# Second unit's gate remainder on GpSimd, first down weights one place sooner, first code products of the extra units behind a gate/up product

## Chip, cores and metric

The kernel runs on 1 core of one Trainium2 chip. The metric is the device time in microseconds of one execution; for a kernel it is the median of its runs.

## What is computed

One layer of a hybrid encoder on x (1, 512, 1024) in float32: RMSNorm, one input projection, a chunked gated delta rule and a sliding-window attention beside each other, a gated merge with output projection and residual, then a mixture of experts. The change lies in the mixture:

```python
grp_prob = jax.nn.softmax(t @ w_rg + b_rg); grp_p, grp_idx = lax.top_k(grp_prob, 1)
top_logits, top_local = lax.top_k(in_group, TOP_K_IN_GROUP)        # 4 groups of 4 experts, 2 experts a token
weights = grp_p * jax.nn.softmax(top_logits, axis=-1)
for gi in range(N_EXPERT_GROUPS):
    act = jax.nn.silu(t @ w_gate[e]) * (t @ w_up[e])                # D_FF_EXPERT = 256
    out = out + (act * combine[:, e, None]) @ w_down[e]
```

followed by the residual and a last RMSNorm.

## The kernel before

Every float32 product is made of three products of rounded parts: a high part (fp32r, copied by ScalarE) and a remainder (raw less high, by VectorE). `three` (lines 1713 to 1716) issues hi·hi, lo·hi and hi·lo, so a weight tile is of use to TensorE (PE) only when ScalarE has made its high part and VectorE (DVE) its remainder.

**Units.** The experts' work is cut into UNITS = 23 units of up to 128 tokens: the 16 experts' first tokens, and 7 extra units for experts with more than 128. `SEQ` gives their order; the first four are experts 0 to 3. For a unit u the kernel gathers its tokens (`fetch`, line 722, GpSimd's queue, an indirect DMA of 128 rows), turns them (`unit_in`, line 2130, PE), splits them (`split_in_hi` on ScalarE, `split_in_lo` on DVE, line 1582), multiplies by gate and up (`gate_up`, 24 products of 128x512), applies SiLU (ScalarE) and the product with up (DVE, line 1634), turns the hidden values (`hidden_f`), splits them (lines 1085 and 1645), and multiplies by down (`down`, 12 products). The loop is a pipeline written out by hand: PE's place u holds unit_in(u+1), the first half of gate_up(u), hidden_f(u-1), the second half of gate_up(u), down(u-1).

**Weights.** Each of a unit's three matrices comes in two loads of 512 KB into a ring of eight raw slots (`ew_raw`). `place` gives a matrix its place c in the order of loads (gate 0, up 0, gate 1, up 1, gate 2, down 0, up 2, gate 3, down 1, ...) and from it the slot and a running count. A load into a slot waits until the remainder of what lay there is made: `elo_done` counts the remainders in the order of the places. SyncE (SP) issues the loads of the 16 experts in program order; GpSimd gathers those of the extra units by row numbers that the routing yields.

**Routing.** Between the residual and the first unit stands the routing, on DVE in small steps chained by a semaphore each. For batches of experts it builds one-hot rows (`one_hots`, line 1550), PE multiplies them with token codes (`row_codes`, line 2110), and DVE turns the result into row numbers (`row_ids`, lines 1557 and 1558). Batches 0 to 4 are the experts (`EARLY` = 5), batches 5 to 8 the extra units, which are made inside the unit loop: `extra_units` in DVE's place 0, `row_codes(5)` to `row_codes(8)` in PE's places 1 to 4 ahead of gate_up(u).

Behind `row_ids(3)` DVE forms the tokens' weights in five small instructions (lines 1572 to 1578), then `row_ids(4)`, then:

```python
1580            split_expert_lo(KIND_G, 1)
...
1626            split_in_lo(0)
1627            split_expert_lo(KIND_U, 1)
```

and in the loop, at place u: the product with up of unit u-1, the remainder of gate u+1, split_in_lo(u+1), (place 0: extra_units), the remainder of down u-1, hidden_lo, the remainder of up u+1, and at places 1 to 4 `row_ids` and `one_hots` of the extra batches.

Of the kernel before, what the change touches and what calls it, by code (L numbers as in the profile page):

```python
# [14 lines left out]
F32 = mybir.dt.float32  # L15
# [67 lines left out]
def build(nc, a, out):  # L83
# [14 lines left out]
    with ctx:  # L98
# [267 lines left out]
        pool_set = sem("gpsimd_set")  # L366
        IDENT_SET, CONSTS, DIST_SET, ROUTE_CONSTS, ZERO_SET, SUB_DONE = range(1, 7)
        choice_step = sem("choice_step")
# [110 lines left out]
        for c in range(3 * UNITS):  # L479
            if c < 4:  # L480
                owner = c // 2
            elif c >= 3 * UNITS - 2:
                owner = c - 2 * UNITS
            else:
                owner = ((c + 2) // 3, (c - 5) // 3, c // 3)[(c + 2) % 3]
            for half in range(2):
                n = 2 * c + half
                LOADS.append((owner, n % EXPERT_RING))
# [19 lines left out]
        def place(kind, u, half=1):  # L508

            if kind == KIND_G:  # L510
                c = 3 * u - 2 if u > 1 else 2 * u
            elif kind == KIND_U:
                c = 3 * u if u > 1 else 2 * u + 1
            else:
                c = 3 * u + 5 if u < UNITS - 2 else 3 * UNITS - (UNITS - u)
            n = 2 * c + half
            return n % EXPERT_RING, (16 if SEQ[u] < NE else 32) * LOADS[n], n + 1

        def halves(gu, kind):
# [37 lines left out]
        def _(sp):  # L557
# [58 lines left out]
            def load(kind, u):  # L616
                if SEQ[u] >= NE:
                    return
                for half in range(2):
                    slot, _, count = place(kind, u, half)  # L620
                    if count > EXPERT_RING:

                        sp.wait_ge(elo_done, count - EXPERT_RING)
                    src = (w_gate_v, w_up_v, w_down_v)[kind][SEQ[u]]
                    src = src[:, half, :] if kind == KIND_D else src[:, UH * half:UH * (half + 1)]
                    sp.dma_start(eraw[slot][:, :], src).then_inc(eraw_in[slot], 16)
# [4 lines left out]
            for t in range(TT):  # L631
                if t < TT - 1:
                    sp.wait_ge(t_scaled, t + 1)
                else:
                    sp.wait_ge(choice_exp, ROW_SCALED)
                sp.dma_start(h_rows[t * P:(t + 1) * P, :], tx[t][:, :]).then_inc(rows_out, 16)
            for u in range(1, UNITS - 1):
                load(KIND_G, u + 1)
                load(KIND_D, u - 1)
                load(KIND_U, u + 1)  # L640
# [16 lines left out]
        def _(pool):  # L657
# [75 lines left out]
            def load_extra(kind, u):  # L733
# [5 lines left out]
                for half in range(2):  # L739
                    slot, _, count = place(kind, u, half)  # L740
                    pool.wait_ge(elo_done, count - EXPERT_RING)
                    c = 2 * (kind == KIND_D) + half
                    nc.gpsimd.indirect_dma_start(
                        out=eraw[slot][:, :], out_offset=None, in_=weight_rows[kind],
                        in_offset=bass.IndirectOffsetOnAxis(ap=wix[:, x_, c:c + 1], axis=0),
                        bounds_check=2 * P * NE - 1, oob_is_err=False).then_inc(extra_in[slot // 2], 16)
# [9 lines left out]
            pool.wait_ge(rows_out, 16 * TT)  # L756
            for u in range(4):
                fetch(u)
            for u in range(UNITS):
# [18 lines left out]
        def _(act):  # L778
# [285 lines left out]
            for u in range(UNITS + 1):  # L1064
# [11 lines left out]
                if u == 0:  # L1076
                    act.wait_ge(tt_ps, WEIGHTS_TURNED)
                    act.activation(w12_f[:, :], ps[1][0:2 * TT, 0:P], ACT.Copy).then_inc(choice_exp, 1)
                    act.wait_ge(choice_exp, WEIGHTS_COPIED)
                    act.dma_start(wt_rows[:, :].rearrange("(r p) o -> r (p o)", p=P), w12_f[:, :]).then_inc(slots_out, 16)  # L1080
                if u:
                    if u < UNITS:
                        split_expert(KIND_D, u - 1)
# [20 lines left out]
        def _(dve):  # L1104
# [474 lines left out]
            row_ids(4)  # L1579
            split_expert_lo(KIND_G, 1)  # L1580

# [47 lines left out]
            for u in range(UNITS + 1):  # L1629
                if u:  # L1630
                    dve.wait_ge(gsilu, u)
                    if u >= 3:
                        dve.wait_ge(hidt_ps, u - 2)
                    dve.tensor_tensor(ea[(u - 1) % 2][:, :], eg[:, :], ps[(u - 1) % 2][:, FF:], ALU.mult).then_inc(hid_done, 1)
                if 0 < u < UNITS - 1:
                    split_expert_lo(KIND_G, u + 1)
# [4 lines left out]
                if u:  # L1641
                    if u < UNITS:
                        split_expert_lo(KIND_D, u - 1)
# [68 lines left out]
        def _(pe):  # L1712
# [444 lines left out]
            def down(u):  # L2157
                pe.wait_ge(elo_done, place(KIND_D, u)[2])
                pe.wait_ge(hid_lo, u + 1)
# [13 lines left out]
            for u in range(UNITS):  # L2173
# [5 lines left out]
                if u == 1:  # L2179
                    pe.wait_ge(choice_exp, WEIGHTS_COPIED)  # L2180
                if 1 <= u <= 4:
                    row_codes(EARLY + u - 1)
                pe.wait_ge(elo_done, place(KIND_U, u)[2])
                pe.wait_ge(xs_lo_done, u + 1)
# [3 lines left out]
                if u:  # L2188
                    hidden_f(u - 1)
                gate_up(u, range(KT // 2, KT))  # L2190
                if u:
                    down(u - 1)
# [46 lines left out]
```

## Time and profile before

| | us |
|---|---|
| median of 3 runs (681.89 to 683.1) | 682.11 |
| the profiled execution's own time | 682.08 |
| its span, from the first to the last instruction | 680.4 |
| TensorE (PE) busy | 652.1 (96%) |
| VectorE (DVE) busy | 477.3 (70%) |
| ScalarE (ACT) busy | 397.7 (58%) |
| GpSimd (POOL) busy | 170.6 (25%) |

The shares are means over the whole span. The routing starts at 416.5 us of the trace and the units run from 430.9 to about 658 us. All places in time below are microseconds from the span's start.

### The profile page before, as it was taken

The numbers are of one execution on the slowest core, as the hardware profiler recorded it, in microseconds if no ns is written. First come the engines' busy times: TensorE is split into PE (matmuls) and PEld (weight loads), VectorE is DVE, ScalarE is ACT, GpSimd is POOL, SyncE is SP. The second block draws the span as 40 slices with busy tenths as digits, with TensorE's granted clock in tenths as the row PEclk, the third lists the DMA queues.
The fourth block names the chain that finished last, engine by engine and source line by source line (L and its number), as shares of the span: only waits on it lengthen the run. The fifth ranks groups of instructions, "written<-read, shape, count | busy, mean of one in ns | idle before, by whom it ended". The sixth has DMA issues, their size and how long they took to land.

```text
span 680.4 us, 9400 instructions
## 1 busy us (share of the span) xinstructions
PE 652.1 (96%) x3421; PEld 543.7 (80%) x3421; DVE 477.3 (70%) x801; ACT 397.7 (58%) x675; POOL 170.6 (25%) x217
## 2 busy tenths in 40 slices
PE   5999999999999999999999998889999999999985
PEld 4788878788888888888888886778888888888763
DVE  5788995264632435424674637999999999998877
ACT  7448584255633332334452356277898889898853
POOL 7000008992000000000000000324647546556100
PEclk9999999999999999999999999789999999999999
DMA  8557534213222211111314904658687887885663
GB/s 267 183 154 203 126 99 134 63 62 79 67 63 64 63 63 62 63 63 63 123 63 159 395 26 164 223 171 260 217 272 214 298 268 237 297 254 181 230 266 124
DMA packets 75840, 108.51 MB, mean 159 GB/s; under 512 B 31767, under 2 KB 53344, under 8 KB 75666
## 3 DMA queue, kind: packets, MB, share of 16 engines
q1 hardware_dynamic: 63232, 99.76, 44.9%
q0 software_dynamic: 12448, 8.11, 4.0%
q8 instruction: 27, 0.44, 0.3%
q14 instruction: 19, 0.16, 0.1%
q10 hardware_dynamic: 114, 0.04, 0.0%
HBM read 123.90 MB, written 20.98 MB: 213 GB/s over the span
## 4 chain that ended last, share of the span: by engine, by line
PE 86%; DVE 8%; DMA 2%; ACT 2%; issue 1%; SPq 0%; POOLq 0%; DVEq 0%; ACTq 0%
PE bank L1714 22%; PE bank L1716 22%; PE bank L1715 22%; PE bank L2138 3%; PE bank L1866 2%; DMA expert_rows<-expert_rows_hbm 1%; PE bank L1772 1%; PE bank L2056 1%; PE bank L1885 1%; PE bank L1925 1%; PE bank L1935 1%; DVE rank_onehot L1550 1%; PE bank L1898 1%; PE bank L1721 1%; DVE gate_up_lo L1434 1%
## 5 line engine op out<-in xcount | busy, mean ns | idle before, releaser
L1714 PE MATMUL bank<-h_hi,w_hi 128*128 128x512 f32 x304 | 123.8, 407 | 1.3 <-DVE h_lo L1137 1.3
L1716 PE MATMUL bank<-h_hi,w_lo 128*128 128x512 f32 x304 | 118.8, 391 | 0.0
L1715 PE MATMUL bank<-h_lo,w_hi 128*128 128x512 f32 x304 | 118.5, 390 | 0.0
L1434 DVE TENSOR_TENSOR gate_up_lo<-ew_raw,gate_up_hi 128x1024 fp32r<-128x1024 f32 x92 | 108.4, 1219 | 5.2 <-ACT gate_up_hi L999 5.0
L728 POOL DMA_INDIRECT unit_tokens<-ffn_rows,row_index x23 | 29.2, 1271 | 277.7 <-DVE row_index L1558 266.1
L1115 DVE TENSOR_TENSOR w_lo<-w_raw,w_hi 128x2048 fp32r<-128x2048 f32 x26 | 59.8, 2299 | 48.6 <-ACT w_hi L790 48.5
L999 ACT ACTIVATE gate_up_hi<-ew_raw 128x1024 fp32r<-128x1024 f32 x92 | 91.9, 1052 | 0.0
L1714 PE MATMUL bank<-gate_up_hi,unit_in_hi 128*128 128x512 f32 x184 | 76.6, 416 | 0.3 <-DVE unit_in_lo L1585 0.3
L1716 PE MATMUL bank<-gate_up_hi,unit_in_lo 128*128 128x512 f32 x184 | 72.6, 395 | 0.0
L1715 PE MATMUL bank<-gate_up_lo,unit_in_hi 128*128 128x512 f32 x184 | 72.5, 394 | 0.0
L1714 PEld LDWEIGHTS bank<-h_hi,w_hi 128*128 128x128 f32 x304 | 57.2, 188 | 13.1 <-issue 2.3
L1716 PEld LDWEIGHTS bank<-h_hi,w_lo 128*128 128x128 f32 x304 | 57.1, 188 | 12.3
L1715 PEld LDWEIGHTS bank<-h_lo,w_hi 128*128 128x128 f32 x304 | 57.3, 188 | 10.7 <-issue 0.5
L790 ACT ACTIVATE w_hi<-w_raw 128x2048 fp32r<-128x2048 f32 x26 | 49.7, 1910 | 16.0 <-PE bank L1716 16.0
L1434 DVE TENSOR_TENSOR down_lo<-ew_raw,down_hi 128x1024 fp32r<-128x1024 f32 x44 | 51.9, 1221 | 4.9 <-ACT down_hi L999 3.0
L714 POOL TENSOR_TENSOR sub_product<-sub_low,sub_inv 128x496 f32<-128x496 f32 (+30 forms) x31 | 26.7, 862 | 88.5 <-DMA sub_low<-chunk_low_hbm 86.1
L999 ACT ACTIVATE down_hi<-ew_raw 128x1024 fp32r<-128x1024 f32 x44 | 44.6, 1079 | 0.0
L1716 PEld LDWEIGHTS bank<-gate_up_hi,unit_in_lo 128*128 128x128 f32 x184 | 35.0, 190 | 7.9
L1714 PEld LDWEIGHTS bank<-gate_up_hi,unit_in_hi 128*128 128x128 f32 x184 | 35.2, 191 | 6.7 <-issue 0.8
L1715 PEld LDWEIGHTS bank<-gate_up_lo,unit_in_hi 128*128 128x128 f32 x184 | 35.2, 191 | 6.1
L1714 PE MATMUL bank<-down_hi,hidden_hi 128*128 128x512 f32 x88 | 34.3, 390 | 0.3 <-issue 0.3
L1716 PE MATMUL bank<-down_hi,hidden_lo 128*128 128x512 f32 x88 | 34.4, 391 | 0.0
(381 smaller groups left out, 1317.8 us busy)
## 6 DMA issues: line engine op xcount, KB each, us to landing
w_raw<-in_w_in SPq DMA_DIRECT2D x16, 1024.0 KB, 5.3
ew_raw<-in_w_gate SPq DMA_DIRECT2D x32, 512.0 KB
ew_raw<-in_w_up SPq DMA_DIRECT2D x32, 512.0 KB
ew_raw<-in_w_down SPq DMA_DIRECT2D x32, 512.0 KB
expert_rows_hbm<-sub_product SPq DMA_DIRECT2D x16, 256.0 KB
w_raw<-in_w_out SPq DMA_DIRECT2D x4, 1024.0 KB, 5.1
expert_rows<-expert_rows_hbm SPq DMA_DIRECT2D x8, 512.0 KB, 7.4
x_T<-in_x SPq DMA_DIRECT2D x4, 512.0 KB, 5.4
```

The costliest lines, as they stand in the source:

```text
L714: link(nc.gpsimd.tensor_tensor(sub_t[:, j + 1:, :], sub_l[:, j + 1:, j:j + 1].broadcast_to(w), sub_x[:, j:j + 1, :].broadcast_to(w), ALU.m ...
L728: nc.gpsimd.indirect_dma_start(out=xg[u % 2][:, :], out_offset=None, in_=h_rows[:, :], in_offset=bass.IndirectOffsetOnAxis(ap=ridx[:, c, 1 ...
L790: act.activation(whi[u % RING][:, :], raw[u % RING][:, :], ACT.Copy).then_inc(hi_done, 1)
L999: act.activation(dst[half], eraw[slot][:, :], ACT.Copy).then_inc(ehi_done, 1)
L1115: dve.tensor_tensor(wlo[s][:, :], raw[s][:, :], whi[s][:, :].bitcast(F32), ALU.subtract).then_inc(lo_done, 1)
L1434: dve.tensor_tensor(dst, eraw[slot][:, :], hi.bitcast(F32), ALU.subtract).then_inc(elo_done, 1)
L1550: dve.tensor_tensor(hot[b % 2][:, :, 0:w], row_rep[:, :, 0:w], bc_mid(col, P), ALU.is_equal).then_inc(hot_done, 1)
L1714: pe.matmul(out_ap, lhs_hi, rhs_hi, start=first, stop=False)
L1715: pe.matmul(out_ap, lhs_hi, rhs_lo, start=False, stop=False)
L1716: return pe.matmul(out_ap, lhs_lo, rhs_hi, start=False, stop=last)
L1866: ins = pe.matmul(o, qb[d, h, m * P:(m + 1) * P], kb[d, m * P - P + c0:(m + 1) * P], start=True, stop=True)
L2138: ins = pe.transpose(bank4(turn_bank_of(u, k // 4))[:, k % 4, :], xg[u % 2][:, :].rearrange("p (c k) -> p k c", k=KT)[:, k, :], ident[:, :])
```

## The change

Four edits. (1) The two remainders of gate 1 go from DVE (line 1580) to GpSimd, between its second and third gather of tokens; they count on GpSimd's own semaphore `pool_set`, so every count of `elo_done` behind them is less by 2 (`lo_count`), and the loads of up 2, which reuse their slots, wait for GpSimd (`slot_free`). (2) Down 0 and gate 2 trade places in the order of loads. (3) Down 0 is split sooner: its high part in ScalarE's place 0, ahead of the first SiLU, and its remainder on DVE in place 1 ahead of that of gate 2, no longer behind split_in_lo(2). (4) `row_codes(5)` moves behind gate_up(1).

```diff
@@ in the order of loads
+            elif c in (4, 5):
+                owner = 2 * (c - 4)
@@ def place
-            if kind == KIND_G:
+            if (kind, u) in ((KIND_D, 0), (KIND_G, 2)):
+                c = 4 + u // 2
+            elif kind == KIND_G:
@@
+        def lo_count(count):
+            return count - 2 if count > 6 else count
+        def slot_free(eng, count):
+            if count in (EXPERT_RING + 5, EXPERT_RING + 6):
+                eng.wait_ge(pool_set, SECOND_GATE_LO + count - EXPERT_RING - 5)
+            else:
+                eng.wait_ge(elo_done, lo_count(count - EXPERT_RING))
@@ gpsimd
-            for u in range(4):
-                fetch(u)
+            def gate_lo(u):
+                for half in range(2):
+                    slot, _, count = place(KIND_G, u, half)
+                    pool.wait_ge(ehi_done, count)
+                    nc.gpsimd.tensor_tensor(halves(gu_lo[u % 2], KIND_G)[half], eraw[slot][:, :],
+                                            halves(gu_hi[u % 2], KIND_G)[half].bitcast(F32), ALU.subtract).then_inc(pool_set, 1)
+            fetch(0)
+            fetch(1)
+            gate_lo(1)
+            fetch(2)
+            fetch(3)
@@ scalar, place u
                     act.dma_start(wt_rows[:, :].rearrange("(r p) o -> r (p o)", p=P), w12_f[:, :]).then_inc(slots_out, 16)
+                    split_expert(KIND_D, 0)
                 if u:
-                    if u < UNITS:
+                    if 1 < u < UNITS:
                         split_expert(KIND_D, u - 1)
@@ vector, behind the routing and at place u
             row_ids(4)
-            split_expert_lo(KIND_G, 1)
...
+                if u == 1:
+                    split_expert_lo(KIND_D, 0)
                 if 0 < u < UNITS - 1:
                     split_expert_lo(KIND_G, u + 1)
...
-                    if u < UNITS:
+                    if 1 < u < UNITS:
                         split_expert_lo(KIND_D, u - 1)
@@ tensor, place u
-                if 1 <= u <= 4:
+                if 2 <= u <= 4:
                     row_codes(EARLY + u - 1)
-                pe.wait_ge(elo_done, place(KIND_U, u)[2])
+                pe.wait_ge(elo_done, lo_count(place(KIND_U, u)[2]))
+                if u == 1:
+                    pe.wait_ge(pool_set, SECOND_GATE_LO_2)
...
                 gate_up(u, range(KT // 2, KT))
+                if u == 1:
+                    row_codes(EARLY)
```

How the instructions stand on the engines, at three places.

GpSimd behind the routing: its gathers of tokens for units 0 to 3 (`unit_tokens`), before:

```order
L728 DMA unit_tokens_143<-ffn_rows,row_index 128x1024 [waits row_index_done,ffn_rows_out]
L728 DMA unit_tokens_144<-ffn_rows,row_index 128x1024 [waits row_index_done]
L728 DMA unit_tokens_143<-ffn_rows,row_index 128x1024 [waits unit_in_ps,row_index_done]
L728 DMA unit_tokens_144<-ffn_rows,row_index 128x1024 [waits unit_in_ps,row_index_done]
L743 DMA ew_raw_123<-in_w_gate,extra_weight_rows 128x1024 [waits ew_lo_done,choice_step]
```

and now:

```order
L745 DMA unit_tokens_143<-ffn_rows,row_index 128x1024 [waits row_index_done,ffn_rows_out]
L745 DMA unit_tokens_144<-ffn_rows,row_index 128x1024 [waits row_index_done]
L779 TENSOR_TENSOR gate_up_lo_130<-ew_raw_123,gate_up_hi_128 128x1024 [waits ew_hi_done]
L779 TENSOR_TENSOR gate_up_lo_130<-ew_raw_124,gate_up_hi_128 128x1024 [waits ew_hi_done]
L745 DMA unit_tokens_143<-ffn_rows,row_index 128x1024 [waits unit_in_ps,row_index_done]
L745 DMA unit_tokens_144<-ffn_rows,row_index 128x1024 [waits unit_in_ps,row_index_done]
```

The two remainders stand ahead of the third gather.

DVE from the tokens' weights to the remainder of up 1 (slots 125 and 126), before:

```order
L1577 TENSOR_TENSOR slot_weights<-slot_weights,group_prob 128x4 [waits dve_step]
L1578 TENSOR_TENSOR slot_weights<-slot_weights,logit_gap 128x4 [waits dve_step]
L1557 TENSOR_SCALAR row_index_f<-bank 128x8 [waits row_codes_ps]
L1558 TENSOR_TENSOR row_index<-row_index_f,bank 128x8 [waits dve_step]
L1434 TENSOR_TENSOR gate_up_lo_130<-ew_raw_123,gate_up_hi_128 128x1024 [waits ew_hi_done,row_index_done]
L1434 TENSOR_TENSOR gate_up_lo_130<-ew_raw_124,gate_up_hi_128 128x1024 [waits ew_hi_done]
L1585 TENSOR_TENSOR unit_in_lo_149<-bank,unit_in_hi_147 128x512 [waits unit_in_hi_done] x2
L1434 TENSOR_TENSOR gate_up_lo_130<-ew_raw_125,gate_up_hi_128 128x1024 [waits ew_hi_done]
```

and now:

```order
L1606 TENSOR_TENSOR slot_weights<-slot_weights,group_prob 128x4 [waits dve_step]
L1607 TENSOR_TENSOR slot_weights<-slot_weights,logit_gap 128x4 [waits dve_step]
L1586 TENSOR_SCALAR row_index_f<-bank 128x8 [waits row_codes_ps]
L1587 TENSOR_TENSOR row_index<-row_index_f,bank 128x8 [waits dve_step]
L1613 TENSOR_TENSOR unit_in_lo_149<-bank,unit_in_hi_147 128x512 [waits unit_in_hi_done,row_index_done]
L1613 TENSOR_TENSOR unit_in_lo_149<-bank,unit_in_hi_147 128x512 [waits unit_in_hi_done]
L1463 TENSOR_TENSOR gate_up_lo_130<-ew_raw_125,gate_up_hi_128 128x1024 [waits ew_hi_done]
```

Unit 0's tokens are split directly behind the row numbers.

PE between the turned tokens of unit 2 and gate_up(1), before:

```order
L2138 MATMUL bank<-ident,unit_tokens_143 128x128 x7
L2122 MATMUL bank<-extra_token_codes_268,rank_onehot_177 128x3 [waits rank_onehot_done,choice_exp]
L2122 MATMUL bank<-extra_token_codes_268,rank_onehot_177 128x3 x3
L2122 MATMUL bank<-extra_token_codes_269,rank_onehot_177 128x3 x4
...
L1714 MATMUL bank<-gate_up_hi_128,unit_in_hi_148 128x512 [waits unit_in_lo_done,ew_lo_done]
```

and now, with the place where the code products went:

```order
L2168 MATMUL bank<-ident,unit_tokens_143 128x128 x7
L1744 MATMUL bank<-gate_up_hi_128,unit_in_hi_148 128x512 [waits gpsimd_set,unit_in_lo_done,ew_lo_done,choice_exp]
...
L1746 MATMUL bank<-gate_up_hi_128,unit_in_lo_150 128x512
L2152 MATMUL bank<-extra_token_codes_268,rank_onehot_177 128x3 [waits rank_onehot_done]
...
L1744 MATMUL bank<-down_hi,hidden_hi 128x512 [waits hidden_lo_done,ew_lo_done]
```

gate_up(1) no longer stands behind the wait for the one-hot rows, and waits for GpSimd besides.

## Rows read from the trace of the kernel before

**Rows 1.** Waits of PE, 430 to 640 us: us in total, times, longest.

```profile
PE bank L2122 <- DVE rank_onehot L1550: 1.9, 1, 1.9
```

**Rows 2.** Timeline of PE, places 0 to 3: start, duration, line [idle before, releaser].

```profile
435.07 0.47 PE L1714 MATMUL bank<-gate_up_hi,unit_in_hi 128*128 128x512 f32 x1 [0.31 <-DVE unit_in_lo L1585]
...
440.99 1.16 PE L2138 MATMUL bank<-ident,unit_tokens 128*128 128x128 f32 x8 [0.20 <-DMA unit_tokens<-ffn_rows,row_index]
444.06 1.13 PE L2122 MATMUL bank<-extra_token_codes,rank_onehot 128*128 128x3 bf16 x16 [1.91 <-DVE rank_onehot L1550]
445.05 0.76 PE L1714 MATMUL bank<-gate_up_hi,unit_in_hi 128*128 128x512 f32 x1
...
452.43 0.39 PE L1714 MATMUL bank<-down_hi,hidden_hi 128*128 128x512 f32 x1
...
456.04 1.10 PE L2122 MATMUL bank<-extra_token_codes,rank_onehot 128*128 128x3 bf16 x16
456.99 0.48 PE L1714 MATMUL bank<-gate_up_hi,unit_in_hi 128*128 128x512 f32 x1
...
466.43 1.10 PE L2122 MATMUL bank<-extra_token_codes,rank_onehot 128*128 128x3 bf16 x16
```

**Rows 3.** Stretches: length, PE busy (instructions), granted clock, DMA share, GB/s.

```profile
441.68:445.10 3.42, 1.51 (x22) 1.00 0.34 138
445.10:448.50 3.40, 3.40 (x10) 0.50 0.51 166
```

**Rows 4.** Timeline of DVE, same columns.

```profile
428.33 1.23 DVE L1550 TENSOR_TENSOR rank_onehot<-index_row_repeated,rank_of_chosen 128x2048 bf16<-128x2048 bf16 x1
...
430.70 0.16 DVE L1577 TENSOR_TENSOR slot_weights<-slot_weights,group_prob 128x4 f32<-128x4 f32 x1
...
431.37 2.36 DVE L1434 TENSOR_TENSOR gate_up_lo<-ew_raw,gate_up_hi 128x1024 fp32r<-128x1024 f32 x2
433.64 1.28 DVE L1585 TENSOR_TENSOR unit_in_lo<-bank,unit_in_hi 128x512 fp32r<-128x512 f32 x2
...
450.30 0.42 DVE L1645 TENSOR_TENSOR hidden_lo<-bank,hidden_hi 128x256 fp32r<-128x256 f32 x1 [0.31 <-ACT hidden_hi L1085]
451.25 2.36 DVE L1434 TENSOR_TENSOR gate_up_lo<-ew_raw,gate_up_hi 128x1024 fp32r<-128x1024 f32 x2 [0.52 <-ACT gate_up_hi L999]
...
453.91 1.23 DVE L1550 TENSOR_TENSOR rank_onehot<-index_row_repeated,extra_rank 128x2048 bf16<-128x2048 bf16 x1
...
464.27 1.23 DVE L1550 TENSOR_TENSOR rank_onehot<-index_row_repeated,extra_rank 128x2048 bf16<-128x2048 bf16 x1
```

**Rows 5.** Timeline of ACT: unit 0's tokens and its SiLU.

```profile
432.88 1.09 ACT L1044 ACTIVATE unit_in_hi<-bank 128x512 fp32r<-128x512 f32 x2 [8.32 <-PE bank L2138]
...
440.83 0.38 ACT L1069 ACTIVATE gate_silu<-bank 128x256 f32<-128x256 f32 x1 [3.40 <-PE bank L1716]
```

**Rows 6.** Timeline of POOL: the gathers of units 1 and 2.

```profile
427.91 1.00 POOL L728 DMA_INDIRECT unit_tokens<-ffn_rows,row_index  x1 [0.31 <-issue]
433.67 0.99 POOL L728 DMA_INDIRECT unit_tokens<-ffn_rows,row_index  x1 [4.76 <-PE bank L2138]
```

**Rows 7.** Groups of POOL by form: busy us, mean ns | idle before.

```profile
L716 POOL TENSOR_TENSOR sub_inv<-sub_inv,sub_product 128x496 f32<-128x496 f32 x1 | 1.3, 1264 | 0.1
...
L716 POOL TENSOR_TENSOR sub_inv<-sub_inv,sub_product 128x256 f32<-128x256 f32 x1 | 0.7, 726 | 0.1
```

**Rows 8.** Timeline of POOL and DVE beside each other, 138 to 152 us.

```profile
138.63 0.68 POOL L714 TENSOR_TENSOR sub_product<-sub_low,sub_inv 128x272 f32<-128x272 f32 x1
138.68 0.65 DVE L1293 TENSOR_TENSOR sink_term<-sinks_b,score_max 128x4 f32<-128x4 f32 x1
...
144.53 2.28 DVE L1115 TENSOR_TENSOR w_lo<-w_raw,w_hi 128x2048 fp32r<-128x2048 f32 x1
144.66 2.56 POOL L714 TENSOR_TENSOR sub_product<-sub_low,sub_inv 128x208 f32<-128x208 f32 x1
...
152.06 0.15 DVE L1293 TENSOR_TENSOR sink_term<-sinks_b,score_max 128x4 f32<-128x4 f32 x1
```

More of the change, by code:

```diff
@@ L366, in build @@
         pool_set = sem("gpsimd_set")
-        IDENT_SET, CONSTS, DIST_SET, ROUTE_CONSTS, ZERO_SET, SUB_DONE = range(1, 7)
+        IDENT_SET, CONSTS, DIST_SET, ROUTE_CONSTS, ZERO_SET, SUB_DONE, SECOND_GATE_LO, SECOND_GATE_LO_2 = range(1, 9)
         choice_step = sem("choice_step")
@@ L621, in load @@
                     if count > EXPERT_RING:
-                        sp.wait_ge(elo_done, count - EXPERT_RING)
+                        slot_free(sp, count)
                     src = (w_gate_v, w_up_v, w_down_v)[kind][SEQ[u]]
@@ L636, in _ @@
                 sp.dma_start(h_rows[t * P:(t + 1) * P, :], tx[t][:, :]).then_inc(rows_out, 16)
+            load(KIND_D, 0)
             for u in range(1, UNITS - 1):
                 load(KIND_G, u + 1)
-                load(KIND_D, u - 1)
+                if u > 1:
+                    load(KIND_D, u - 1)
                 load(KIND_U, u + 1)
@@ L740, in load_extra @@
                     slot, _, count = place(kind, u, half)
-                    pool.wait_ge(elo_done, count - EXPERT_RING)
+                    slot_free(pool, count)
                     c = 2 * (kind == KIND_D) + half
@@ L2157, in down @@
             def down(u):
-                pe.wait_ge(elo_done, place(KIND_D, u)[2])
+                pe.wait_ge(elo_done, lo_count(place(KIND_D, u)[2]))
                 pe.wait_ge(hid_lo, u + 1)
```

## The prediction

> **What bounds the kernel now.** The busy shares come first: PE is busy 96% of the span, so a change helps only where PE stands idle or its clock is low. I then read PE's waits over the units' stretch: from 430 to 640 us the list has one large entry, 1.9 us for the one-hot rows of the first extra code products [rows 1]. The timeline of PE shows where [rows 2]: unit 2's tokens are turned at 440.99, then PE idles 1.91 us until 444.06, runs 16 narrow products, and starts gate_up(1) at 445.05. The stretches add what the waits can't show [rows 3]: behind 441.68 to 445.10, in which PE was busy 1.51 of 3.42 us and did nearly only turns and narrow products, the granted clock is 0.50 (1.2 of 2.4 GHz) up to 448.50. gate_up(1) with hidden_f(0) in it lasts 445.05 to 452.43, 7.4 us; gate_up(0) lasts 435.07 to 440.79 (the start of the turns less their 0.20 idle), 5.7 us, and hidden_f adds 0.15. The low clock costs about **1.5 us**.
>
> The last view is the timeline of DVE, since the one-hot rows are DVE's [rows 4]. From 433.64 it has no idle time up to 449.99, where it waits 0.31 and then 0.52 us for ScalarE. Afterwards it is nearly as full as PE: the one-hot rows of the next extra batches start at 453.91 and 464.27, 10.36 us apart, while PE's code products start at 456.04 and 466.43, 10.39 us apart [rows 2, 4]. So between places 2 and 4 DVE leads PE by only 0.8 us (464.27 + 1.23, and 0.14 from DVE's end to PE's start, against 466.43). Whatever PE gains in place 1, it keeps no more than that plus what DVE gains.
>
> **The change, part by part.**
>
> *Code products behind gate_up(1).* They wait for nothing there. Taken alone this removes 1.91 us of idle time and the low clock behind it.
>
> *Gate 1's remainder leaves DVE.* DVE issues 2.27 us less (431.37 to 433.64) [rows 4]. But its next work, the remainders of unit 0's tokens, needs ScalarE's high parts, the first of which ends at about 433.45 (half of 432.88 + 1.09) [rows 5]. So 2.1 of the 2.27 us become idle time, and taken alone the edit brings 0.15 us to that chain.
>
> *Down 0 sooner.* On ScalarE the two copies fall into 3.40 us of waiting for gate_up(0) [rows 5]; they take some 2 us and cost nothing unless gate_up(0) ended over 1 us sooner. On DVE the same number of remainders stands ahead of hidden_lo(0) as before. What goes is DVE's idle 0.31 + 0.52 us: hidden_f(0) and up 2's high part come sooner with PE. With 0.15 from above, DVE's place 2 would come 1.0 us sooner. The loads of down 0 and gate 2 both start at free slots before the routing ends; their order costs nothing.
>
> *The remainders on GpSimd, their length.* GpSimd has no 128x1024 subtraction in this trace. Its own subtraction takes 726 ns for 256 and 1264 ns for 496 elements [rows 7], 2.24 ns an element, so 1264 + 528 x 2.24 = **2.45 us** each. The lower bound is DVE's 1.2 us [rows 4]; the upper is 2.45 plus a full DVE instruction of waiting, about 4.7. I take 2.45, since it is the same operation on the same engine. The Trainium skill (GPSIMD Engine Reference, Elementwise) measures 4497 ns for 2048 elements; as an estimate that is 2.25 us each, and the sum below would be 0.4 us lower.
>
> *Their start and whom they hold up.* The second gather ends at 428.91 [rows 6], and DVE makes one-hot rows, with two inputs in SBUF, until about 429.5 [rows 4]. The delta rule's rows show that such instructions and GpSimd's exclude each other [rows 8]: a DVE product-like instruction of 4 elements took 0.65 us where it takes 0.15, ending with GpSimd's (138.63 + 0.68), and a GpSimd multiplication that began 0.13 us behind a DVE remainder took 2.56 us, ending after it. So GpSimd holds from 429.5 to 431.9 and, 0.1 us later, from 432.0 to 434.45. DVE's L1577 (430.70) has two SBUF inputs and so has L1578, chained behind it; if the first gets its turn between the two remainders, the second comes after both. From L1577 to the end of the row numbers it is 0.67 us (430.70 to 431.37) [rows 4], and L1577 may be through already; I take 0.65. DVE then starts unit 0's remainders at **435.1, not 433.64: 1.45 us later**. Bounds: 0.15 us sooner if nothing excludes, 2.3 later if each remainder took 0.4 longer. The rows show waits of at most about 2 us. The Trainium skill (SBUF — State Buffer, Who interferes with whom) says that the loser "fully blocks" for the whole instruction, which speaks for the full 2.45; a lock handed over in pieces would give the second rival's time.
>
> *Whoever waits behind that.* gate_up(0) starts at 435.1 + 1.2 + 0.1 = 436.4 and ends at 442.1. The third gather starts at about 434.5 and not 433.67 [rows 6]; it landed just before 440.99, 7.3 us after its start, so now at 441.8, hidden. Turns 442.1 to 443.05; gate_up(1) from **443.1** (before 445.05) to 448.9 at full clock; code products 0.95 (456.04 to 456.99) to 449.9. down(0) needs hidden_lo(0): DVE's chain from unit 0's remainders to it is 16.35 us (433.64 to 449.99), so 435.1 + 16.35 + 0.33 = 451.8, and PE starts at 451.9 (before 452.43). DVE's up 2 follows at 451.8 (before 451.25), its next one-hot rows at 454.4 (453.91), and PE's code products can start at 454.4 + 1.15 + 0.14 = 455.7, **0.35 us sooner** than 456.04, at full clock.
>
> *The clock.* From 448.9 to 451.9 PE has the code products and 2 us of idle time, the picture that stood before the low clock of today [rows 3]. I expect the same answer: half clock behind it, at most 1.5 us on down(0) and the turns, of which 0.2 lie in the wait for 455.7. Place 2 then starts up to 0.95 us later than before; less if part of the slow stretch falls on the idle time. I take **0.8 us later**. From there PE waits for nothing and carries it to the end.
>
> **Sum.** Against the profiled execution's own 682.08 us (0.03 below the median of the runs shown): 682.08 + 0.8 = **682.9 us**. About 0.2%, 1.4 us, is what a measurement of this kernel can tell from no change.
>
> **The rivals.**
>
> 1. *The clock holds.* For it: idle time and narrow products are split differently, and PE's wide products lie closer around them. Against it: rows 3. Then place 2 starts 0.35 us sooner: 681.7.
>
> 2. *DVE isn't held up.* If GpSimd takes its second remainder late enough to let L1577 and L1578 both through, or no lock counts here, DVE's chain is 1.0 us sooner in place 2, hidden_lo(0) is ready at 450.3 against PE at 448.9, and PE gains 1.0 + 0.8 to 0.9 us: 680.2, faster. For it: the two are very short, and GpSimd's start may shift. Against it: both of rows 8, and that each needs its own turn.
>
> 3. *The third gather comes late*, the slower side. It now stands behind both remainders on GpSimd's queue, and lands beside loads that these release. PE has 2 us of slack in place 1, so it decides from a landing at about 444: PE then idles 2 us ahead of gate_up(1), gets half clock for it (1.5 us), and down(0) starts at 453.8 and not 452.43, place 2 at 457.4: 1.4 us later, 683.5. For it: 7.3 us of landing time, for 0.5 MB, say that the queues are full. Against it: up 2's loads go out before, and gate 3's after it.
>
> 4. *Edits that do nothing:* GpSimd's subtraction near DVE's 1.2 us each. Both then end at 432; DVE isn't late, and the result is that of rival 2.
>
> **Chances.** Forecast 0.48, rival 1 0.22, rivals 2 and 4 together 0.15, rival 3 0.09, and 0.06 for mixtures. Faster by over 0.2% takes rivals 2 and 4 and a little of 1: 0.16. Slower by over 0.2% takes most of rival 3 and the upper edge of the forecast with longer remainders: 0.14. Within 0.2%: 0.70. The range reaches down past rival 1 with shorter remainders (2.1 us each gain 0.7) to 680.9, and up past rival 3 to 683.8.
>
> **What would show it.** L779 (GpSimd) at 2.4 to 2.5 us twice, from about 429.0 with part of the first as waiting; L1606 or L1607 (DVE) ending with them near 434.5 instead of taking 0.16; unit_in_lo at 435.1; gate_up(0) at 436.4 and gate_up(1) at 443.1; PE idle 2 us ahead of down(0) and a granted clock of 0.50 behind it, none at 445. Wrong if L1606 and L1607 both take 0.16 (rival 2), if the clock stays at 1.00 (rival 1), or if the turns of unit 2 wait for the DMA beyond 443 (rival 3).

## The result and the profile after

| | before, us | after, us |
|---|---|---|
| median (lowest to highest) of 19 runs each | 681.89 (679.16 to 684.55) | **686.21** (683.11 to 688.62) |
| the profiled execution's own time | 682.08 | 685.94 |
| its span | 680.4 | 684.2 |

The ratio is 1.0062, with an interval from 1.0049 to 1.0075. The change makes the kernel slower by 4.3 us; the interval gives 3.3 to 5.1. The prediction was 682.9 and its range ended at 683.8: it was wrong. By the profiled executions the loss is 3.86 us. (Line numbers moved: the one-hot rows are L1579 now, the remainders L1463 and on GpSimd L779, PE's code products L2148 and L2152, the turns L2168, gate/up and down L1744.)

The list of PE's waits from 425 to 650 us no longer has the 1.9 us for the one-hot rows of the extra units [rows 1]. At its head stand the one-hot rows of the routing itself: us in total, times, longest. Four such waits were there before too, but with 2.4 us in all and 1.4 at the longest.

```profile
PE bank L2148 <- DVE rank_onehot L1579: 7.5, 4, 5.5
...
PE bank L1744 <- DVE hidden_lo L1675: 1.4, 1, 1.4
```

The timeline of PE of the changed kernel, against [rows 2]:

```profile
428.34 1.15 PE L2148 MATMUL bank<-token_codes,rank_onehot 128*128 128x3 bf16 x16 [0.38 <-DVE rank_onehot L1579]
434.98 1.15 PE L2148 MATMUL bank<-token_codes,rank_onehot 128*128 128x3 bf16 x16 [5.49 <-DVE rank_onehot L1579]
435.99 3.65 PE L2168 MATMUL bank<-ident,unit_tokens 128*128 128x128 f32 x16
440.11 0.76 PE L1744 MATMUL bank<-gate_up_hi,unit_in_hi 128*128 128x512 f32 x1 [0.25 <-DVE unit_in_lo L1613]
...
446.32 1.04 PE L2168 MATMUL bank<-ident,unit_tokens 128*128 128x128 f32 x8
447.12 0.48 PE L1744 MATMUL bank<-gate_up_hi,unit_in_hi 128*128 128x512 f32 x1
...
452.96 1.15 PE L2152 MATMUL bank<-extra_token_codes,rank_onehot 128*128 128x3 bf16 x16
455.51 0.77 PE L1744 MATMUL bank<-down_hi,hidden_hi 128*128 128x512 f32 x1 [1.39 <-DVE hidden_lo L1675]
...
460.66 1.10 PE L2152 MATMUL bank<-extra_token_codes,rank_onehot 128*128 128x3 bf16 x16
```

Batch 3 of the routing's code products (428.34) stands 1.53 us behind batch 2, and in the kernel before so does batch 4 behind batch 3. Here batch 4, the last, comes 6.64 us behind (434.98). DVE and GpSimd show why, against [rows 4, 6]:

```profile
427.06 1.23 DVE L1579 TENSOR_TENSOR rank_onehot<-index_row_repeated,rank_of_chosen 128x2048 bf16<-128x2048 bf16 x1
...
428.59 6.33 DVE L1579 TENSOR_TENSOR rank_onehot<-index_row_repeated,rank_of_chosen 128x2048 bf16<-128x2048 bf16 x1
...
436.07 0.16 DVE L1606 TENSOR_TENSOR slot_weights<-slot_weights,group_prob 128x4 f32<-128x4 f32 x1
436.26 0.16 DVE L1607 TENSOR_TENSOR slot_weights<-slot_weights,logit_gap 128x4 f32<-128x4 f32 x1
...
438.68 1.29 DVE L1613 TENSOR_TENSOR unit_in_lo<-bank,unit_in_hi 128x512 fp32r<-128x512 f32 x2 [1.98 <-ACT unit_in_hi L1072]
```

```profile
428.17 0.99 POOL L745 DMA_INDIRECT unit_tokens<-ffn_rows,row_index  x1 [0.30 <-issue]
429.20 4.64 POOL L779 TENSOR_TENSOR gate_up_lo<-ew_raw,gate_up_hi 128x1024 fp32r<-128x1024 f32 x2
438.77 1.00 POOL L745 DMA_INDIRECT unit_tokens<-ffn_rows,row_index  x1 [4.94 <-PE bank L2168]
```

The same one-hot instruction takes 1.23 us and then 6.33: 5.10 us of waiting that the trace shows as busy time. GpSimd's two subtractions end at 433.84, and 1.08 us later, about its own length, DVE's ends. By its record it had begun 0.61 us *before* the first of them, while the gather still ran (428.17 to 429.16).

**Where the 3.86 us are.** From batch 3's code products to those of place 2, called the stretch from here on, it is 32.32 us (428.34 to 460.66), where before it was 27.96 (428.08 to 456.04): +4.36. Of these +5.11 lie between the last two batches (6.64 for 1.53), and -0.75 behind them. The rest of the span's 3.8 is +0.26 ahead of the stretch and -0.82 behind it. The granted clock is about half of full speed at two places, for long around the wait and briefly behind the wait of down(0), and at 445 it is not:

```profile
428.10:441.70 13.60, 7.62 (x53) 6.79 (x54) 11.28 (x18) 2.75 (x6) 7.86 (x5) 0.51 0.39 122
441.70:455.40 13.70, 12.42 (x71) 10.21 (x70) 13.19 (x30) 10.63 (x14) 0.26 (x1) 0.99 0.56 183
455.40:458.80 3.40, 3.29 (x8) 2.67 (x9) 3.33 (x5) 0.03 (x1) 1.12 (x1) 0.54 0.88 281
```

(Window and length; busy us and instructions of PE, weight loads, DVE, ACT, POOL; granted clock, DMA share, GB/s.) The first of the two is not new. Before, in the same columns, it lasted to 435.00; now it lasts to 441.70 and takes in the first products of gate_up(0), which lasts 6.2 us for 5.7:

```profile
428.10:431.60 3.50, 3.02 (x36) 2.85 (x37) 3.12 (x13) 0.00 (x0) 0.81 (x1) 0.50 0.38 110
431.60:435.00 3.40, 3.16 (x15) 2.66 (x13) 3.40 (x5) 1.50 (x3) 0.99 (x1) 0.52 0.34 104
```

### The profile page after: what moved, and what is told of

Read it like the earlier page. It is cut to its first block, busy times and chain, and to the rows that moved or that the text cites. A ratio compares the mean times of both kernels' runs of the same rounds, so it can differ in the third digit from the quotient of the medians.

```text
span 684.2 us, 9400 instructions
## 1 busy us (share of the span) xinstructions
PE 653.8 (96%) x3421; PEld 544.5 (80%) x3421; DVE 480.5 (70%) x799; ACT 397.7 (58%) x675; POOL 175.1 (26%) x219
## 4 chain that ended last, share of the span: by engine, by line
PE 87%; DVE 8%; DMA 2%; ACT 2%; issue 1%; SPq 0%; POOLq 0%; DVEq 0%; ACTq 0%
PE bank L1744 22%; PE bank L1746 22%; PE bank L1745 22%; PE bank L2168 3%; PE bank L1896 2%; DVE rank_onehot L1579 2%; PE bank L1802 1%; DMA expert_rows<-expert_rows_hbm 1%; PE bank L1955 1%; PE bank L1965 1%; PE bank L1915 1%; PE bank L1928 1%; PE bank L2126 1%; PE bank L1751 1%; PE bank L2086 1%
## 5 line engine op out<-in xcount | busy, mean ns | idle before, releaser
L1744 PE MATMUL bank<-h_hi,w_hi 128*128 128x512 f32 x304 | 123.8, 407 | 1.3 <-DVE h_lo L1166 1.3
L1463 DVE TENSOR_TENSOR gate_up_lo<-ew_raw,gate_up_hi 128x1024 fp32r<-128x1024 f32 x90 | 106.1, 1222 | 5.1 <-ACT gate_up_hi L1027 5.0
L1744 PE MATMUL bank<-gate_up_hi,unit_in_hi 128*128 128x512 f32 x184 | 76.1, 414 | 0.2 <-DVE unit_in_lo L1613 0.2
L1744 PEld LDWEIGHTS bank<-h_hi,w_hi 128*128 128x128 f32 x304 | 57.2, 188 | 13.2 <-issue 2.4
L1463 DVE TENSOR_TENSOR down_lo<-ew_raw,down_hi 128x1024 fp32r<-128x1024 f32 x44 | 51.9, 1222 | 5.0 <-ACT down_hi L1027 3.1
L731 POOL TENSOR_TENSOR sub_product<-sub_low,sub_inv 128x496 f32<-128x496 f32 (+30 forms) x31 | 24.6, 795 | 88.3 <-DMA sub_low<-chunk_low_hbm 86.0
L1744 PEld LDWEIGHTS bank<-gate_up_hi,unit_in_hi 128*128 128x128 f32 x184 | 35.0, 190 | 6.6 <-issue 0.7
L1744 PE MATMUL bank<-down_hi,hidden_hi 128*128 128x512 f32 x88 | 35.0, 398 | 1.4 <-DVE hidden_lo L1675 1.4
```

The costliest lines, as they stand in the source:

```text
L731: link(nc.gpsimd.tensor_tensor(sub_t[:, j + 1:, :], sub_l[:, j + 1:, j:j + 1].broadcast_to(w), sub_x[:, j:j + 1, :].broadcast_to(w), ALU.m ...
L1463: dve.tensor_tensor(dst, eraw[slot][:, :], hi.bitcast(F32), ALU.subtract).then_inc(elo_done, 1)
L1744: pe.matmul(out_ap, lhs_hi, rhs_hi, start=first, stop=False)
```

## The experiments

Theory A: the whole loss is the one-hot rows held by GpSimd's two subtractions, so that edits 2 to 4 alone would win 1 to 2 us. Rival D: the loss lies in the other edits. Rival B: it is the third gather's delay. The column "stretch" is the length from batch 3's code products to place 2's, in the one profiled execution of each kernel.

| kernel | median, us | ratio to before, interval | stretch |
|---|---|---|---|
| before | | | 27.96 |
| the change | 686.21 (19 runs) | 1.0062, 1.0049 to 1.0075 | 32.32 |
| e1, edits 2 to 4 | 682.53 (12) | 1.0002, 0.9986 to 1.0017 | 27.76 |
| e2, edit 4 | 682.47 (12) | 1.0004, 0.9992 to 1.0016 | 27.67 |
| e3, edit 1 | 688.14 (6) | 1.0097, 1.0077 to 1.0118 | 31.14 |
| e4, subtractions behind the row numbers | 684.58 (9) | 1.0048, 1.0028 to 1.0067 | 31.97 |
| e5, behind the one-hot rows | 684.56 (1) | | 27.60 |
| e6, a MEMSET ahead of them | 681.13 (1) | | 27.10 |
| e6b, the same | 683.15 (12) | 1.0003, 0.9988 to 1.0018 | 27.15 |
| e7, each waits for the one before | 683.68 (1) | | 28.60 |
| e8, e1 with two GpSimd MEMSETs | 681.19 (1) | | 28.06 |
| e9, e10 with all four code products behind gate/up | 682.61 (12) | 0.9997, 0.9979 to 1.0016 | |
| e10, e1 with hidden_lo(0) sooner | 682.52 (12) | 0.9993, 0.9977 to 1.0009 | 26.07 |
| e11, e6 with all four behind gate/up | 683.10 (12) | 1.0011, 0.9993 to 1.0029 | |

Before ran at 682.57 beside e1 to e4 (26 runs), 682.22 beside e5 to e8 (one), and 682.76 beside e6b and e9 to e11 (35). The ratio is an estimate of its own and not the quotient of the two medians, which is 1.0082 for e3 and 1.0029 for e4. The stretch has no value for e9 and e11, where place 2's code products stand elsewhere. A time from one run (e5 to e8) says little: single executions of a kernel lie up to 5.4 us apart.

**e1: edits 2 to 4 alone.** DVE keeps gate 1's remainders.

```diff
             fetch(1)
-            gate_lo(1)
             fetch(2)
@@ vector
             row_ids(4)
+            split_expert_lo(KIND_G, 1)
```

(With it go the count in `lo_count` and the two waits on `pool_set`.)

> Edits 2 to 4 without edit 1: the two remainders of gate 1 stay on DVE behind the last row numbers. Theory A (GpSimd's two subtractions hold DVE's one-hot rows of batch 4 for 5.1 us, and that is the whole loss): the one-hot instruction takes 1.23 us again, gate_up(0) starts at 435.1, gate_up(1) at about 442.2 instead of 445.05, down(0) at about 450.4, place 2 some 1.7 us sooner than before; 680.2 to 681 us against 681.9. Rival D (the loss lies in the moved down weights or code products): still 3 us or more slower than before.

**e2: edit 4 alone.** The kernel before with `row_codes(5)` behind gate_up(1).

```diff
-                if 1 <= u <= 4:
+                if 2 <= u <= 4:
                     row_codes(EARLY + u - 1)
...
                 gate_up(u, range(KT // 2, KT))
+                if u == 1:
+                    row_codes(EARLY)
```

> The kernel before with edit 4 alone (the first code products of the extra units behind gate_up(1)). Theory A, and what the prediction said of the moved down weights (same number of remainders on DVE ahead of hidden_lo(0)): within 0.5 us of e1, so 680.2 to 681.5 us. Rival: the earlier down weights carry the gain; then this one is within 0.5 us of the kernel before.

**e3: edit 1 alone.** The changed kernel with the other three edits taken back.

> The kernel before with edit 1 alone (the remainders on GpSimd). Theory A: the one-hot instruction takes 6.3 us, gate_up(0) starts at 440, place 1 keeps its idle time for the code products; 5 to 6.5 us slower than before, 687 to 688.5 us. Rival D: about as fast as before, within 1 us.

Neither e1 nor e2 differs from before, so the half of theory A that promised a gain failed: e1 has 682.53 for the 680.2 to 681 expected, e2 682.47 for 680.2 to 681.5. e3 is slower by 5.6 us between the medians, as expected, and its trace holds the same instruction again:

```profile
430.09 4.64 POOL L773 TENSOR_TENSOR gate_up_lo<-ew_raw,gate_up_hi 128x1024 fp32r<-128x1024 f32 x2
```

```profile
429.49 6.34 DVE L1572 TENSOR_TENSOR rank_onehot<-index_row_repeated,rank_of_chosen 128x2048 bf16<-128x2048 bf16 x1
```

Rival D falls. The intervals of e3 and of the change don't meet, though: beside edit 1 the other edits seem to be worth 1 to 2 us, alone nothing. e3's stretch is 1.2 us shorter than the change's all the same. Its profile is of its fastest run (686.14 against a median of 688.14), and in it no half clock follows PE's wait of 1.71 us for the extra one-hot rows: the granted clock is 1.00 from 449 to 460 us. Whether it follows in e3's other runs isn't known, so what the other edits are worth there stays open.

Why did edit 4 win nothing, when the wait of 1.91 us that it removes is gone from e2's trace?

```profile
447.72 1.15 PE L2122 MATMUL bank<-extra_token_codes,rank_onehot 128*128 128x3 bf16 x16
450.32 0.47 PE L1714 MATMUL bank<-down_hi,hidden_hi 128*128 128x512 f32 x1 [1.46 <-DVE hidden_lo L1645]
...
455.62 1.10 PE L2122 MATMUL bank<-extra_token_codes,rank_onehot 128*128 128x3 bf16 x16
```

```profile
445.00:448.50 3.50, 3.50 (x27) 2.81 (x26) 3.50 (x5) 3.50 (x6) 0.00 (x0) 1.00 0.65 188
451.30:454.70 3.40, 3.40 (x9) 2.59 (x9) 3.33 (x7) 0.00 (x0) 2.20 (x2) 0.53 0.75 224
```

The idle time moved to down(0), which waits for DVE's hidden_lo(0), and the half clock moved from 445 [rows 3] to behind it. Of the 1.91 us the stretch keeps 0.29. e1 shows the same: 1.11 us of idle time ahead of down(0), and a granted clock of 0.51 from 453.4 to 456.8.

**e4: the subtractions wait for the routing's last row numbers**, so GpSimd meets none of the routing's one-hot rows.

```diff
             fetch(1)
+            pool.wait_ge(ids_done, 5)
             gate_lo(1)
```

> The changed kernel, but GpSimd's two remainders wait for the last row numbers (row_ids(4)). Theory A: they run from 431.4 to 436.0 us, in which DVE has little with two SBUF inputs except up 1's remainder, which starts at 436.0 and not 434.7; the one-hot rows take 1.23 us; DVE's place 2 within 0.5 us of before, PE's up to 1 us sooner; 681 to 682.5 us. Rival B (the third gather, which stands behind the remainders, makes the loss): it starts at 436.1 and not 433.7, half of the changed kernel's delay of 5.1 us, so about 2 us slower than before, 684 us.

The one-hot rows take 1.23 us again, yet the kernel is still slower than before, by 0.48% (2.0 us between the medians), where theory A had expected 681 to 682.5. Another wait took their place:

```profile
435.07 0.47 PE L1745 MATMUL bank<-gate_up_hi,unit_in_hi 128*128 128x512 f32 x1 [0.25 <-DVE unit_in_lo L1614]
...
445.88 1.97 PE L2169 MATMUL bank<-ident,unit_tokens 128*128 128x128 f32 x8 [5.11 <-DMA unit_tokens<-ffn_rows,row_index]
```

```profile
431.51 4.68 POOL L779 TENSOR_TENSOR gate_up_lo<-ew_raw,gate_up_hi 128x1024 fp32r<-128x1024 f32 x2 [2.51 <-DVE row_index L1588]
436.35 1.81 POOL L745 DMA_INDIRECT unit_tokens<-ffn_rows,row_index  x1 [0.16 <-issue]
```

This is the prediction's third rival, real here: the third gather goes out at 436.35, 2.7 us later than before [rows 6], and its rows are there 9.5 us behind that, where they took 7.3. In the changed kernel it goes out later still (438.77), but gate_up(0) is as late, and the turns at 446.32 wait for nothing. So rival B is no part of the change's loss; it is what this plain wait brought in its stead.

**e5: the subtractions wait for the row numbers of batch 3** (`ids_done` 4 for 5), which DVE has ready 1.5 us before those that e4 waits for. **e6: a MEMSET of two columns**, chained by GpSimd's semaphore, stands ahead of them:

```diff
             fetch(1)
+            link(nc.gpsimd.memset(l_w[:, :], 0.0))
             gate_lo(1)
```

**e7: each subtraction is followed by a wait for its own end**, so that the second is not issued while the first runs. Instructions of DVE and GpSimd that exclude each other take turns on what the recorded texts call the shared pair. e6 and e7 are to tell theory L (the turn goes to the instruction that was issued first, and the first subtraction was issued while the gather ran, ahead of the one-hot rows) from theory P (GpSimd takes the turn whenever it comes). The trace shows when an instruction started, not when it was issued.

> The changed kernel, but GpSimd's remainders wait for the row numbers of batch 3, which DVE makes right behind the one-hot rows of batch 4. The one-hot rows take 1.23 us. Theory A with the prediction's handover: the remainders start near 429.9, DVE's tensor-scalar and the two products of the tokens' weights have to wait for them (one of these instructions takes 2 us or more), unit 0's remainders start near 435. If only instructions over some length were held, those small ones take 0.16 us.

> The changed kernel with a short chained memset of 128x2 between the second gather and the remainders, so that the first subtraction is dispatched only when gather and memset are through, with DVE's one-hot instruction already running. Theory L (the shared pair goes to the instruction dispatched first; in the changed kernel the subtraction was dispatched while the gather still ran, ahead of the one-hot rows): one-hot rows 1.23 us, the first remainder starts behind them. Theory P (GpSimd takes the pair whenever it comes): one-hot rows again over 5 us.

> The changed kernel with a wait on the first remainder's own count ahead of the second. Theory A with handover between instructions: the one-hot rows wait for the first remainder alone, some 3.7 us instead of 6.3, and the second remainder waits for them (3.3 us instead of 2.3). If the two hold the pair together whatever stands between them: 6.3 us again.

In e5 the one-hot rows take 1.23 us, and small instructions behind them wait, as theory A expected. Two instructions that take 0.17 and 0.16 us without GpSimd beside them take 2 us each:

```profile
432.62 2.02 DVE L1605 TENSOR_SCALAR slot_weights<-logit_gap 128x4 f32<-128x4 f32 x1
434.89 2.06 DVE L1607 TENSOR_TENSOR slot_weights<-slot_weights,group_prob 128x4 f32<-128x4 f32 x1
```

GpSimd and DVE of e6:

```profile
429.18 0.12 POOL L784 MEMSET late_weights<- 128x2 f32 x1
429.39 4.99 POOL L779 TENSOR_TENSOR gate_up_lo<-ew_raw,gate_up_hi 128x1024 fp32r<-128x1024 f32 x2
434.53 1.01 POOL L745 DMA_INDIRECT unit_tokens<-ffn_rows,row_index  x1 [0.15 <-issue]
```

```profile
428.61 1.22 DVE L1580 TENSOR_TENSOR rank_onehot<-index_row_repeated,rank_of_chosen 128x2048 bf16<-128x2048 bf16 x1
430.56 1.53 DVE L1605 TENSOR_SCALAR slot_weights<-logit_gap 128x4 f32<-128x4 f32 x1
432.13 0.18 DVE L1606 RECIPROCAL slot_weights<-slot_weights 128x4 f32<-128x4 f32 x1
432.34 2.06 DVE L1607 TENSOR_TENSOR slot_weights<-slot_weights,group_prob 128x4 f32<-128x4 f32 x1
```

The subtraction starts 0.19 us later than in the changed kernel, at 429.39 and still inside the one-hot rows, and now it is GpSimd that waits: 4.99 us for the two instead of 4.64, while DVE's keeps its 1.22. A 0.12 us instruction turned the order round. Theory P falls; theory L fits e6, its repeat e6b and e11, and e7 below. That the first subtraction of the changed kernel was issued during the gather is inferred from this and not seen: the MEMSET also put it 0.19 us later. The gather itself doesn't hold the one-hot rows, for in the kernel before they take 1.23 us beside it [rows 4, 6]. Behind the one-hot rows DVE is held about where the prediction had seen it: L1605 to the end of the first subtraction, L1607 to the end of the second.

DVE and the two forms of GpSimd's line in e7 (count, shortest, median and longest in ns, first and last start):

```profile
429.30 4.05 DVE L1580 TENSOR_TENSOR rank_onehot<-index_row_repeated,rank_of_chosen 128x2048 bf16<-128x2048 bf16 x1
```

```profile
L779 POOL TENSOR_TENSOR gate_up_lo<-ew_raw,gate_up_hi x2: 2351/2800/3249, 429.9 to 432.3; 128x1024 fp32r<-128x1024 f32 x2
```

The one-hot rows now wait 2.82 us, for one subtraction, get in, and the second (3.25 us) waits for them, much as expected (3.7 us for the one-hot rows, 3.3 for the second). So the hold of 5.1 us needed both: two subtractions with no wait between them kept the turn, over the waiting one-hot rows. They don't keep it from every instruction: in e6 the TENSOR_SCALAR (L1605) gets in between two that stand just as close.

> The change with one small GpSimd MEMSET of two columns ahead of the two GpSimd subtractions, timed in rounds where the single look gave 681.13. Theory L (the lasting loss of the change is the one-hot rows of batch 4, held 5.1 us because the first subtraction had been issued while the gather ran): with the one-hot rows at 1.23 us the rest of the change is left: place-2 codes come 25.6 after the last code products, against 26.4 before, so 681.7 us where before has 682.5 (ratio 0.998 to 1.000), and about 4.5 us less than the change itself. Rival D (the loss lies in the other three edits or in the late first remainder): near 686.

e6b tests the sum. With one instruction more the change loses nothing: 1.0003, for an expected 0.998 to 1.000, where the change itself has 1.0062. What it does not do is win, although its stretch is 0.8 us shorter than before. 681.13, the single run of e6, was luck, and the two profiles show where most of it lies: e6b reaches the stretch at 430.55 us and e6 at 428.37, and e6b has about half clock from 44.0 to 47.5 us (0.53), where e6 has 1.00. In both the half clock also lasts longer than before (up to 441 us in e6), and gate_up(0) takes 7.7 and 7.8 us for 5.7.

**e8: which work of GpSimd counts.** e1 with two MEMSETs of 128x1024 where the subtractions stood; PE waits for them.

> The remainders of gate 1 on DVE again (edits 2 to 4 kept), and at the place between the second and third gather two GpSimd memsets of 128x1024 in the buffers of the units' results, which read nothing from SBUF. Theory R (DVE instructions with two SBUF inputs collide with GpSimd's reads only, as the Trainium skill's SBUF page states): one-hot rows 1.23 us, about as e1. Rival: any GpSimd instruction holds them up, and they take about 1.2 us plus the memsets' time.

```profile
428.46 0.98 POOL L781 MEMSET unit_out<- 128x1024 f32 x1
429.35 0.98 POOL L782 MEMSET unit_out<- 128x1024 f32 x1
```

```profile
427.89 1.22 DVE L1577 TENSOR_TENSOR rank_onehot<-index_row_repeated,rank_of_chosen 128x2048 bf16<-128x2048 bf16 x1
429.84 0.53 DVE L1602 TENSOR_SCALAR slot_weights<-logit_gap 128x4 f32<-128x4 f32 x1
```

The first MEMSET begins inside the one-hot rows, and neither is longer for it. Only the TENSOR_SCALAR is (0.53 for 0.17), and it ends with the second MEMSET. So a GpSimd instruction that only writes didn't hold one with two inputs in SBUF; the subtractions, which read as well, did.

**e9 to e11: can edits 2 to 4 be made to pay?** Theory C: they gave nothing because of the idle time ahead of down(0) and the half clock behind it. Rival Q: the half clock falls somewhere in any case. e10 is e1 with hidden_lo(0) computed directly behind down 0's remainder, ahead of gate 2's; e9 is e10 with all four extra units' code products behind gate/up; e11 is e6 with that.

```diff
                 if u == 1:
                     split_expert_lo(KIND_D, 0)
+                    hidden_remainder(u)
```

> e1 with unit 0's hidden_lo ahead of gate 2's remainders on DVE and nothing else. Theory C: the idle time of 1.1 us ahead of down(0) goes, and the half clock behind it: 1 to 2.5 us less than e1, 680.5 to 681.5. Rival Q: idle gone, but the half clock falls elsewhere in the stretch: 681.5 to 682.5.

> DVE keeps the second gate's remainders (as e1); all four extra units' code products stand behind gate/up, and unit 0's hidden_lo is computed as soon as down 0's remainder is done, ahead of gate 2's. Theory C (edits 2 to 4 gave nothing in e1 because the 1.1 to 1.4 us that PE no longer idled ahead of the codes came back as idle time ahead of down(0), with half clock behind it): without that idle time 680.5 to 681.5 (ratio 0.997 to 0.999). Rival Q (the clock falls once in this stretch wherever the narrow code products stand, so nothing is won): 682.5, within 0.1%.

> The change with the GpSimd MEMSET ahead (as e6) and the code products of all four extra units behind gate/up, where the change moves only the first unit's. At places 2 to 4 no PE idle time stands ahead of the codes in e6, so both theories expect the same time as e6b within 0.1%; if the codes behind gate/up keep the clock up at those places too, 0.5 to 1.5 us less than e6b.

e10's PE in place 2:

```profile
448.10 0.47 PE L1746 MATMUL bank<-down_hi,hidden_hi 128*128 128x512 f32 x1
...
450.96 1.05 PE L2170 MATMUL bank<-ident,unit_tokens 128*128 128x128 f32 x8
453.34 1.15 PE L2154 MATMUL bank<-extra_token_codes,rank_onehot 128*128 128x3 bf16 x16 [1.33 <-DVE rank_onehot L1575]
```

The wait ahead of down(0) is gone, and PE waits 1.33 us for DVE's next one-hot rows instead. Its stretch is 1.9 us shorter than before's, and still 12 runs give 682.52, 0.07% under before, with no change inside the interval; e9 gives 682.61 and e11 683.10. By its trace e10 is what theory C described (a granted clock of 1.00 from 440 to 457 us), by its time what rival Q did (681.5 to 682.5 expected, where theory C had 680.5 to 681.5). No version beats the kernel before.

Why a shorter stretch doesn't show in the medians is only partly known. A stretch is that of one execution, and not of a typical one: the profiled executions of e3, e9 and e10 were the fastest of their runs, that of e1 (685.17) its slowest, and runs of before alone lie 5.4 us apart. Executions also differ far ahead of the stretch. e1 reaches it 2.6 us later than before, and all of that is lost before 417 us: the turns at 416.65 us in the kernel before stand at 419.24. A window of e1 in which before has a granted clock of 1.00 shows part of it:

```profile
44.00:47.50 3.50, 3.50 (x11) 2.75 (x10) 3.43 (x4) 0.41 (x1) 0.00 (x0) 0.55 0.00 0
```

## Why the prediction was wrong

**The step that failed is "Their start and whom they hold up".** It let GpSimd's first subtraction begin "from 429.5", once the one-hot rows were through, because they were running when it was due. The start of GpSimd's record was taken for the time from which it counts in the order. In the changed kernel it came first although DVE's record starts at 428.59 and its own at 429.20, and in e6, with one instruction in between, it came second. That fits an order by issue, with the subtraction issued while GpSimd's gather ran. So it was not L1577 that waited (L1606 in the changed kernel, 0.16 us) but the last one-hot rows, and the delay was 5.10 us and not 1.45; and those rows are on PE's path through the code products, the row numbers, unit 0's tokens and gate_up(0) (440.11, forecast 436.4). L1606 and L1607 at 0.16 us were the prediction's sign of rival 2, a faster kernel; the sign came, but because the hold had fallen on an earlier instruction. e6 comes near the kernel that was forecast: DVE starts unit 0's remainders at 434.90 (forecast 435.1) and PE gate_up(0) at 436.34 (436.4).

The Trainium skill (SBUF — State Buffer, Who interferes with whom) was quoted for the loser "fully blocks". The runs agree: the one-hot rows got nothing done in 5.10 us and 2.82 us of waiting. But 5.10 us is longer than one instruction of GpSimd's. The same section says that issue order decides; the prediction read "issue" as the start in the trace. It also says that an instruction with two inputs in SBUF contends with GpSimd's reads alone, and that TENSOR_SCALAR has modes that can contend with GpSimd whatever it does: e8 agrees with both (1.22 us beside a MEMSET, and 0.53).

The other steps, by the same rows:

- *The length of GpSimd's subtractions*: 2.32 us each, for 2.45. Right.
- *gate_up(0) to down(0)*: forecast 15.5 us (436.4 to 451.9), measured 15.40 (440.11 to 455.51). Before it was 17.36. Right.
- *The clock*: forecast half clock behind the idle time ahead of down(0), none at 445. Both are in the rows above. down(0) to place 2's codes: forecast 4.9 us, measured 5.15. Right, and e2 shows it for edit 4 alone. It was no certainty: in e7 PE idled 1.67 us at the same place and the granted clock stayed at 1.00 (453 to 460 us). The half clock that stood at 428.1 to 435.0 already was in no step; the delay drew it out to 441.7.
- *Idle ahead of down(0)*: 2 us forecast, 1.39 measured.
- *Edits 2 to 4 win little*: e1, 1.0002. Right, as far as e1 can say, for it leaves edit 1 out.
- *Rival 3*: not in the changed kernel, where everything PE does is as late as the gather, but in e4 with 5.11 us of idle time, where 2 us had been priced.

With the failed term alone replaced the sum comes out near the result: 1.35 us of delay at gate_up(0) was in it, and the trace has 5.04 (440.11 for 435.07). 682.9 + 3.7 = 686.6, against 685.94 and a median of 686.21. It is 0.7 us over, and behind place 2, where the forecast had no change, the changed kernel wins 0.82. The exclusion that decided was in the sum, but on the wrong instruction and at 1.45 us instead of 5.10.

## What to carry to other kernels

Work that reads SBUF and is moved to GpSimd can cost DVE its whole length. Which DVE instruction pays is not to be read from the starts in a trace: here one paid that had started 0.61 us earlier. Look for DVE instructions with two inputs in SBUF around the place, take GpSimd's whole run of such instructions as the possible delay of each, and ask which of them is on the path. If one is, something short ahead of GpSimd's work (e6) or a wait between its parts (e7) may move or shorten the hold; here the first took the whole loss away. A wait for DVE's results (e4) did not, because the gather behind it went out late. And where a wait is taken away ahead of DVE-fed work, look for the next wait on the same feeder before counting a gain.

## What the runs showed of the hardware

- An instruction on GpSimd held one on DVE that had started 0.61 us before it, for 5.10 us (6.33 for 1.23), and two of GpSimd's in a row kept their turn; in e7, where the second waited for the end of the first, the hold was 2.82 us. But in e6 a TENSOR_SCALAR that waited through the first subtraction was let in at the switch (it ended at 432.09, the first subtraction at 432.07). What decides at the switch is open.
- The same gather took 7.3 us to land before and 9.5 us in e4, where it went out 2.7 us later.
- The length of PE's idle time didn't decide whether half clock followed. Around the 16 narrow code products it did behind 1.11 us (e1), 1.39 (the changed kernel), 1.46 (e2), 1.91 (before), 1.95 (e8) and 1.96 (e11). It did not behind 1.33 (e10), 1.67 (e7) and 1.71 (e3). In e10 the idle time ends at 453.34, and the granted clock behind it is 1.00:

```profile
455.40:458.80 3.40, 3.40 (x18) 2.77 (x17) 3.40 (x5) 1.21 (x2) 1.22 (x2) 1.00 0.74 242
```
